# Quarter score products inside a level, and the last z projection one turn earlier, in a hybrid decoder block

## Chip, cores, metric

One NeuronCore of a Trainium2 chip. The time is the device time of one execution of the kernel in microseconds; the value before is the median of 3 runs.

## Reference, cut to what matters

One decoder layer (512 tokens, width 1024, 8 heads per mixer, all float32):

```python
proj = rmsnorm(x) @ w_in                      # q, k, v of both mixers, z, gates
# mixer A, per head: two score maps of 64-wide halves j of q and k
logits[j] = qa[:, j] @ ka[:, j].T + bias      # causal
w = softmax(logits[0]) - lam * softmax(logits[1])
oa = rmsnorm(w @ va)
# mixer B, per head: chunked gated delta rule, chunk 64
#   A = I + strict_lower(k k^T * decay); its inverse is applied, then a scan over chunks
ob = rmsnorm(delta_rule(qb, kb, vb)) * silu(zb)
mixed = sigmoid(g0) * (oa @ w_br_a) + sigmoid(g1) * (ob @ w_br_b)
x = x + mixed @ w_out
# then a gated MLP with a width-3 convolution, and a gated embedding term
```

## The kernel before

Every projection is a `gemm` of one 128-column chunk of weights. Weights and activations are each split into a high and a low part, so each of the 8 blocks of the inner dimension takes three products of 512 columns (L498). These three products are one **fill step**; a chunk is 8 steps. Weights stream through four buffers: SP loads a chunk, GpSimd (`both`) or ScalarE (`high`) makes the high part, GpSimd (`split`) the low part. All chunks stand in one fixed order (`Stream`), and each has a fixed PSUM bank out of four.

The mixers are worked off in **turns**. `turn(h)` does head h of mixer B (`delta`) and head h+1 of mixer A (`attention`), and as fill the projections that later turns need. `turn(-1)` has no `delta`. Turns 0 to 5 are the **middle turns** (both mixers, and projections for another head of A: `more_a`); turn 6 is the **late turn** (nothing more of A to project), turn 7 the **last turn** (no attention). Each engine has its own copy of the turn's order, written out by hand; semaphores join them. TensorE's copy places fill steps with `f.step(n)`, and the tuples `STEPS...` say how many go where: `early` (before the levels), `first` and `second` (within and behind a level), `scan`, `late`.

A turn on TensorE, in order:
- `scores(a, 0)` (L602), the products k k^T (L648) and q k^T (L657), `ob_sum` of the head before (L631), `turn_w(a, 0)` (L609), `scores(a, 1)`.
- Six **levels** n = 1 to 6 that double the size of the inverted blocks. Each has a product of 64x64 tiles (L678, at n = 6 L680) into bank 7, which ScalarE copies to `ui` (L1072), and a second product from `ui` and `xt` (L690, at n = 6 L692), from which VectorE makes the next `xi` (L1484) and, transposed, the next `xt` (L1487). `first[n-1]` fill steps stand between the two, `second[n-1]` behind the second.
- Behind levels 2 and 4: `turn_w` of the attention weights, one step, the next `scores`. Behind level 6: `k_turn` (L626).
- `v_mm` (L712), `turn_w(a, 3)`, `v_turn` (L590), and a scan of four token tiles (L723, L724, L727, L732, L735), with `attend` (L616) after the first tile and `oa_sum` (L743) after the third. Then the sums for q and k of the next head but one (L572).

The attention of one head goes through its four token tiles i one after the other, because its scores, their softmax and the transposed weights share banks 3 and 4: `scores` i on TensorE; `maxima` on VectorE (bias, L1355; row extremes, L1360); `softmax` on ScalarE (L959); `combine` on VectorE (L1370 to L1372), which makes `pr`; `turn_w` on TensorE; `keep_w` on ScalarE (L965), which makes `wT`, for which the next `scores` waits. `scores` i uses (i+1)*128 columns, twice: once with rows 0 to 63 of q and k, once with rows 64 to 127.

Other names: `vbt` (L1501) is the scaled value tile, made on VectorE at level 2; SiLU is finished on VectorE in L1401; `conv` is L1386 and L1390; `o_a` (L1554) ends a head of A; `finish_z` is L1574; `prep` (L1345) makes `qa` and `ka`; `ob_scaled` is signalled by L1565. The late turn has four chunks of fill (`LATE`). The last turn has `zb` of head 7 as its first chunk (`LAST`), then eight chunks of `mix_a`, the gated branch projections of mixer A; before it TensorE waits for all of `o_a` (`oa_done`).

## Time and profile before

| | |
|---|---|
| time, median of 3 runs | 1237.29 us (1236.37 to 1237.43) |
| the profiled execution | 1236.77 us, its span 1235.0 us |
| TensorE (PE) busy | 97% of the span |
| VectorE (DVE), ScalarE (ACT), GpSimd (POOL) busy | 56%, 44%, 50% |
| chain that ended last | PE 82%, DVE 10%, ACT 5% |
| DMA | 83 GB/s on the mean |

The middle turns run from 104.1 to 505.3 us, the late turn to 561.1, the last turn's scan ends at 628.2; then come the rest of the branch projections, the output projection, the MLP and the embedding term. PE is TensorE's matmul queue and PEld its weight loads. Float32 matmuls show two records each. A record's duration reaches past the start of the next one, since matmuls are pipelined: what a product costs is read from one start to the next start.

### The profile page before, as it was taken

What the parts mean: (1) busy time and instruction counts of PE and PEld (TensorE: products, weight loads), DVE (VectorE), ACT (ScalarE), POOL (GpSimd) and SP (SyncE); (2) the same over time, 40 slices, a digit from 0 to 9 for tenths busy, and PEclk for the clock granted to TensorE, in tenths of its full rate; (3) what the DMA queues carried; (4) which work ended last, traced back from release to release, by engine and by line L of the source; (5) the groups of instructions that cost most, each with busy time, mean ns of one, the idle gap of its engine ahead of it and who ended that gap; (6) DMA issues with size and microseconds to landing.
All of it is one profiled execution on the core that took longest, in us unless ns stands there. A gap on an engine that the chain in (4) does not pass through costs nothing.

```text
span 1235.0 us, 19086 instructions
## 1 busy us (share of the span) xinstructions
PE 1194.4 (97%) x6526; PEld 933.7 (76%) x6526; DVE 689.4 (56%) x1157; ACT 541.8 (44%) x926; POOL 615.8 (50%) x764
## 2 busy tenths in 40 slices
PE   5989999999999999989999999999999999999998
PEld 3766776767676777767788888888888888888886
DVE  4276667685858586777330242446677722751534
ACT  4254554555554645455242222454444422432542
POOL 5644354445343453425535564456666664574552
PEclk9989999999999999999999999999999999999999
DMA  8231212221212112211214352233433342332223
GB/s 256 76 95 53 61 52 61 69 61 53 61 52 78 52 35 78 69 35 52 69 51 120 85 176 79 86 93 94 120 94 94 101 121 69 102 100 87 66 84 89
DMA packets 192403, 102.65 MB, mean 83 GB/s; under 512 B 3798, under 2 KB 191177, under 8 KB 192329
## 3 DMA queue, kind: packets, MB, share of 16 engines
q1 hardware_dynamic: 191948, 101.55, 28.9%
q8 instruction: 41, 0.67, 0.2%
q14 instruction: 33, 0.27, 0.1%
q10 hardware_dynamic: 381, 0.15, 0.0%
HBM read 99.57 MB, written 2.13 MB: 82 GB/s over the span
## 4 chain that ended last, share of the span: by engine, by line
PE 82%; DVE 10%; ACT 5%; issue 2%; DMA 1%; SPq 0%; DVEq 0%; ACTq 0%
PE bank L498 68%; PE bank L602 2%; PE bank L678 2%; PE bank L690 1%; PE bank L616 1%; ACT junk_k L1040 1%; DVE qb L1401 1%; PE bank L609 1%; ACT silu L977 1%; PE bank L648 1%; PE bank L657 1%; ACT silu L978 1%; DVE ast L1360 1%; PE bank L631 1%; DVE ct L1414 1%
## 5 line engine op out<-in xcount | busy, mean ns | idle before, releaser
L435 POOL TENSOR_TENSOR w_lo<-w_raw,w_hi 128x256 fp32r<-128x256 f32 x692 | 543.7, 819 | 268.0 <-ACT w_hi L876 262.4
L498 PE MATMUL bank<-hn_hi,w_hi 128*128 128x512 f32 x1000 | 423.2, 423 | 0.0
L498 PE MATMUL bank<-hn_hi,w_lo 128*128 128x512 f32 x1000 | 391.9, 392 | 0.0
L498 PE MATMUL bank<-hn_lo,w_hi 128*128 128x512 f32 x1000 | 391.2, 391 | 0.0
L450 POOL CAST w_hi<-w_raw 128x1024 fp32r<-128x1024 f32 x68 | 72.2, 1062 | 334.7 <-PE bank L498 322.2
L498 PEld LDWEIGHTS bank<-hn_hi,w_hi 128*128 128x128 f32 x1000 | 188.4, 188 | 48.0 <-issue 11.2
L498 PEld LDWEIGHTS bank<-hn_hi,w_lo 128*128 128x128 f32 x1000 | 188.0, 188 | 41.2
L498 PEld LDWEIGHTS bank<-hn_lo,w_hi 128*128 128x128 f32 x1000 | 188.8, 189 | 37.1 <-issue 6.5
L876 ACT ACTIVATE w_hi<-w_raw 128x1024 fp32r<-128x1024 f32 x113 | 120.0, 1062 | 74.8 <-PE bank L498 66.6
L1689 DVE SCALAR_TENSOR_TENSOR u<-vr,pt,u 128x511 f32<-128x511 f32 x88 | 89.4, 1016 | 8.0 <-DVE vr L1683 0.3
L1683 DVE TENSOR_TENSOR vr<-bank,rs 128x512 f32<-128x512 f32 x44 | 30.4, 692 | 72.2 <-PE bank L498 67.1
L498 PE MATMUL bank<-fa_hi,w_hi 128*128 128x512 f32 x176 | 68.5, 389 | 0.0
L498 PE MATMUL bank<-fa_lo,w_hi 128*128 128x512 f32 x176 | 68.5, 389 | 0.0
L498 PE MATMUL bank<-fa_hi,w_lo 128*128 128x512 f32 x176 | 68.5, 389 | 0.0
L1206 ACT ACTIVATE u<-vr,pt 128x512 f32<-128x512 f32 x44 | 35.9, 816 | 38.4 <-DVEq L1684 37.6
L1072 ACT ACTIVATE ui<-bank 128x256 f32<-128x256 f32 (+1 forms) x48 | 18.4, 384 | 62.4 <-PE bank L678 56.1
L1723 DVE TENSOR_TENSOR x<-x,bank 128x512 f32 x16 | 11.0, 688 | 61.2 <-PE bank L498 60.5
L959 ACT ACTIVATE pr<-bank,ast 128x128 f32<-128x128 f32 (+3 forms) x64 | 33.8, 528 | 23.1 <-DVE ast L1360 21.1
L965 ACT ACTIVATE wT<-bank 128x128 f32<-128x128 f32 (+3 forms) x32 | 14.0, 438 | 67.9 <-PE bank L609 67.9
L1211 ACT ACTIVATE fa_hi<-tn 128x512 fp32r<-128x512 f32 x22 | 13.9, 633 | 65.6 <-DVE tn L1701 65.6
L678 PEld LDWEIGHTS bank<-xi,ct 64*64 64x64 f32 x640 | 22.0, 134 | 25.2 <-issue 14.0
L1626 DVE TENSOR_TENSOR sg<-sg,bank 128x512 f32<-128x512 f32 x8 | 5.5, 687 | 61.6 <-PE bank L498 61.6
(277 smaller groups left out, 1771.2 us busy)
## 6 DMA issues: line engine op xcount, KB each, us to landing
w_raw<-in_w_in SPq DMA_DIRECT2D x73, 512.0 KB, 3.9
w_raw<-in_w_up SPq DMA_DIRECT2D x44, 512.0 KB, 3.8
w_raw<-in_w_down SPq DMA_DIRECT2D x16, 512.0 KB, 3.9
w_raw<-in_w_br_a SPq DMA_DIRECT2D x8, 512.0 KB, 4.0
w_raw<-in_w_br_b SPq DMA_DIRECT2D x8, 512.0 KB, 3.9
w_raw<-in_w_out SPq DMA_DIRECT2D x8, 512.0 KB, 4.1
w_raw<-in_w_ple_gate SPq DMA_DIRECT2D x8, 512.0 KB, 4.1
w_raw<-in_w_down SPq DMA_DIRECT2D x8, 384.0 KB, 3.4
```

The costliest lines, as they stand in the source:

```text
L435: ins = pool.tensor_tensor(wlo[c.slot][:, ks, :], raw[c.slot][:, ks, :], whi[c.slot][:, ks, :].bitcast(F32), ALU.subtract)
L450: pool.tensor_copy(whi[c.slot][:, :, :], raw[c.slot][:, :, :]).then_inc(high_ready, 1)
L498: mm = pe.matmul(acc, w[c.slot][:, i, :], xx[:, x0 + i, :], start=(i == 0 and n == 0), stop=last)
L602: mm = pe.matmul(bank[3 + j][:, 0:(i + 1) * P], qa[s, i * P:(i + 1) * P], ka[s, 0:(i + 1) * P], start=True, stop=True)
L678: mm = pe.matmul(packed(7, 0, t, q), ct[n % 2][q, t, :], xi[q, t, :], start=True, stop=True)
L876: done(nc.scalar.activation(whi[c.slot][:, :, :], raw[c.slot][:, :, :], ACT.Copy), high_ready, c.number + 1)
L959: done(nc.scalar.activation(pr[j][:, 0:w], bank[3 + j][:, 0:w], ACT.Exp, bias=ast[:, 2 + j:3 + j], scale=-1.0, accum_out=ast[:, 4 + j:5 + j]),
L965: done(nc.scalar.activation(wT[:, 0:i + 1, i * P:(i + 1) * P], tiles(3)[:, 0:i + 1, :], ACT.Copy), "a_wT", h * 4 + (i + 1))
L1072: done(nc.scalar.activation(ui[q, :, :], packed(7, part=q), ACT.Copy), "ui", h * (NL - 1) + n)
L1206: done(nc.scalar.activation(u[:, :], v[:, :], ACT.Identity, bias=col(PA_FBIAS + q * KF, f), scale=col(PA_TAP[2] + q * KF, f)), "u_made", 2 ...
L1683: done(V.tensor_tensor(v[:, :], bank[c.bank][:, :], rs[:, :], ALU.mult), bank_free[c.bank], c.uses + 1)
L1689: link(V.scalar_tensor_tensor(out=u[:, back:], in0=v[:, 0:T - back], scalar=col(PA_TAP[j] + q * KF, f), in1=u[:, back:], op0=ALU.mult, op1 ...
```

## The change

In turns with both `delta` and `more_a` (named `tight`: turns 0 to 5), `scores` of token tiles 1, 2 and 3 stand between the two products of levels 1, 3 and 5, where fill steps stood, and each row half of a score is done as two products of 64 output partitions (`quarters`). The fill steps of that place go behind the second product. The softmax steps on ScalarE and VectorE move behind by about a level; `turn_w(a, 3)`, `v_turn`, `attend` and `oa_sum` move one scan tile back. `STEPS` gives four more steps behind levels 2 and 4 and four fewer at the turn's end.

The z projection of head 7 becomes a fifth chunk of the late turn (`zl`); `LAST` goes. The last turn's fill begins with `mix_a`, whose bank order becomes 2, 1, 3, 0; eight steps of a ninth chunk follow around `ob_sum`. TensorE's wait for `oa_done` ahead of the last turn goes. Of `mix_a`, GpSimd casts two more chunks and ScalarE two fewer. `low_a` does six blocks ahead of level 1, not four.

```diff
-STEPS = ((3, 2, 1, 1, 2), (2,) * 6, (1, 1, 1, 1, 1, 1), (3, (1, 1), (1, 1, 1), (1, 1, 1), (1, 1, 1)), (3, 6))
+STEPS = ((3, 2, 1, 1, 2), (2,) * 6, (1, 3, 1, 3, 1, 1), (3, (1, 1), (1, 1, 1), (1, 1, 1), (1, 1, 1)), (2, 3))
...
-STEPS_LATE = ((4, 2, 1, 1, 2), (2,) * 6, (0, 0, 0, 0, 0, 0), (2, (1, 0), (1, 0, 1), (1, 0, 1), (1, 0, 1)), (0, 0))
-STEPS_LAST = ((4, 4, 4, 2, 2), (3,) * 6, (3, 3, 3, 3, 3, 3), (3, (1, 1), (1, 1, 2), (1, 1, 2), (1, 1, 2)), (0, 0))
+STEPS_LATE = ((3, 2, 1, 1, 2), (2,) * 6, (1, 1, 1, 1, 1, 2), (3, (1, 0), (1, 0, 1), (1, 1, 1), (1, 1, 1)), (0, 1))
+STEPS_LAST = ((5, 2, 2, 2, 2), (3,) * 6, (3, 3, 3, 3, 3, 2), (2, (1, 1), (1, 1, 2), (1, 1, 1), (1, 1, 1)), (0, 0))
...
-LATE = ("qb", "kb", "vb", "zb")
-LAST = ("zb",)
+LATE = ("qb", "kb", "vb", "zb", "zl")
 HEAD_BANKS = (1, 0, 2)
-AHEAD = {"qa": 2, "ka": 2, "va": 2, "qb": 1, "kb": 1, "vb": 1, "zb": 0}
+AHEAD = {"qa": 2, "ka": 2, "va": 2, "qb": 1, "kb": 1, "vb": 1, "zb": 0, "zl": 1}
...
-        self.mix_a = Segment(self, KD // 2, slots, [2, 1, 0, 3])
+        self.mix_a = Segment(self, KD // 2, slots, [2, 1, 3, 0])
...
-            for n in range(4):
+            for n in range(len(LATE)):
                 both(stream.late.at(n))
-            both(stream.last.at(0))
-
-            for n in range(8 + 3):
+
+            for n in range(13):
                 both(stream.mix_a.at(n))
-            split(stream.mix_a.at(8 + 3))
-            for n in range(12, 16):
+            for n in range(13, 16):
...
+            def scores(h, i, quarters=False):
...
-                for j in range(2):
-                    s = slice(64 * j, 64 * j + 64)
-                    mm = pe.matmul(bank[3 + j][:, 0:(i + 1) * P], qa[s, i * P:(i + 1) * P],
-                                   ka[s, 0:(i + 1) * P], start=True, stop=True)
+                for j, s in enumerate((LOW, UP)):
+                    if not quarters:
+                        mm = pe.matmul(bank[3 + j][:, 0:(i + 1) * P], qa[s, i * P:(i + 1) * P],
+                                       ka[s, 0:(i + 1) * P], start=True, stop=True)
+                    else:
+                        for m, part in enumerate((LOW, UP)):
+                            at = i * P + m * HEAD
+                            mm = pe.matmul(bank[3 + j][part, 0:(i + 1) * P], qa[s, at:at + HEAD],
+                                           ka[s, 0:(i + 1) * P], start=True, stop=True)
                 mm.then_inc(sem("a_scores"), 1)
...
+                tight = delta and more_a
+                if attention and not tight:
                     scores(a, 1)
                 f.step(early[4])
...
                         mm.then_inc(sem("level_u"), 1)
-                    f.step(first[n - 1])
+                    joined = tight and n % 2 == 1
+                    if joined:
+                        scores(a, (n + 1) // 2, quarters=True)
+                    else:
+                        f.step(first[n - 1])
                     if delta:
...
                         mm.then_inc(sem("level_vt"), 1)
-                    f.step(second[n - 1])
+                    f.step(second[n - 1] + (first[n - 1] if joined else 0))
...
                     if n in (2, 4) and attention:
                         turn_w(a, n // 2)
                         f.step(1)
-                        scores(a, n // 2 + 1)
+                        if not tight:
+                            scores(a, n // 2 + 1)
                     if n == 6 and attention:
                         k_turn(a)
...
                 f.step(scan[0])
                 if attention:
-                    turn_w(a, 3)
-                    v_turn(a)
+                    if not tight:
+                        turn_w(a, 3)
+                        v_turn(a)
...
                     f.step(scan[1 + t][1])
-                    if t == 0 and attention:
+                    if t == 0 and tight:
+                        turn_w(a, 3)
+                        v_turn(a)
+                    if t == (1 if tight else 0) and attention:
                         attend(a)
-                    if t == 2 and attention:
+                    if t == (3 if tight else 2) and attention:
                         pe.wait_ge(sem("oa_sq"), a + 1)
                         pe.matmul(bank[4][:, :], ones, pr[1][:, :], start=True, stop=True).then_inc(sem("oa_sum"), 1)
...
-            pe.wait_ge(sem("oa_done"), H + 1)
-            fill = [gemm(stream.last.at(0), hn_hi, hn_lo)]
+            fill = []
             for n in range(2):
                 fill += [gemm(stream.mix_a.at(q, n), hn_hi, hn_lo) for q in range(2)]
                 fill += [gemm(stream.mix_a.at(2 + q, n), oa_hi, oa_lo, ready=("o_split", 0) if n + q == 0 else None)
                          for q in range(2)]
             turn(H - 1, None, fill, attention=False, more_a=False, steps=STEPS_LAST)
+            f = Fill(gemm(stream.mix_a.at(0, 2), hn_hi, hn_lo))
+            f.step(1)
             ob_sum(H - 1)
-
+            f.rest()
+            run(gemm(stream.mix_a.at(1, 2), hn_hi, hn_lo))
+            for q in range(2):
+                run(gemm(stream.mix_a.at(2 + q, 2), oa_hi, oa_lo))
...
-                    softmax(a, 1)
+                    if not tight:
+                        softmax(a, 1)
                 for n in range(1, NL):
+                    if tight and n in (3, 5):
+                        keep_w(a, n // 2)
...
                         if n == 2:
-                            keep_w(a, 1)
+                            if tight:
+                                softmax(a, 1)
+                            else:
+                                keep_w(a, 1)
                             silu_exp(a, 0)
...
                         if n == 4:
+                            if tight:
+                                softmax(a, 2)
                             act.wait_ge(sem("rows_read"), a + 1)
                             done(nc.scalar.activation(dec[:, :, :], dec[:, :, :], ACT.Exp), "dec", a + 1)
-                            keep_w(a, 2)
+                            if not tight:
+                                keep_w(a, 2)
                         if n == 5:
                             silu_exp(a, 1)
-                            softmax(a, 3)
+                            if not tight:
+                                softmax(a, 3)
                         if n == 6:
+                            if tight:
+                                softmax(a, 3)
                             first_tap(a, 2, at("vb"))
...
-                    if n in (1, 3) and not attention:
-                        gate_a(n // 2)
-                    if n == 2 and not attention:
-                        gate_z(h, at("zb"), attention)
+                    if n == 1 and not attention:
+                        gate_z(h, at("zl"), attention)
+                    if n in (2, 3) and not attention:
+                        gate_a(n - 2)
...
-                    high(seg.at(q + 3, n))
+                    if q < own:
+                        high(seg.at(q + 3, n))
+                if own == 0:
+                    act.wait_ge(low_ready, seg.at(5, n).number)
                 for q in range(2, 4):
                     high(seg.at(q + 3, n))
...
-                    low_a(range(4))
-                if attention:
+                    low_a(range(6))
+                if attention and not tight:
                     maxima(a, 1)
...
-                                link(V.transpose(xt[0:32, :, 32:64], xi[32:64, :, 0:32]))
+                                V.transpose(xt[0:32, :, 32:64], xi[32:64, :, 0:32])
                                 done(V.transpose(xt[64:96, :, 32:64], xi[96:128, :, 0:32]), "xt", h * NL + (n + 1))
...
                     if n == 1:
                         if attention:
-                            combine(a, 1)
+                            (maxima if tight else combine)(a, 1)
                             steps(conv(a, 0, at("qb")))
...
                         if attention:
-                            maxima(a, 2)
+                            if tight:
+                                combine(a, 1)
+                            else:
+                                maxima(a, 2)
                             steps(finish_silu(a, 0))
                     if n == 3 and attention:
+                        if tight:
+                            maxima(a, 2)
                         decay(a)
-                        combine(a, 2)
+                        if not tight:
+                            combine(a, 2)
                     if n == 4 and attention:
+                        if tight:
+                            combine(a, 2)
                         steps(conv(a, 1, at("kb")))
-                        maxima(a, 3)
+                        if not tight:
+                            maxima(a, 3)
                     if n == 5 and attention:
+                        if tight:
+                            maxima(a, 3)
                         steps(finish_silu(a, 1))
+                        if not tight:
+                            combine(a, 3)
+                    if n == 6 and tight:
                         combine(a, 3)
                     if n == 6 and h > 0:
                         finish_ob(h - 1)
                     if not attention:
-                        if n in (1, 2):
-                            low_a(range(2 * n + 2, 2 * n + 4))
+                        if n == 1:
+                            low_a(range(6, 8))
                         if n in (4, 5):
                             mix_a(n - 4, stream.mix_a.at(2 + n - 4), sqr[n - 4])
```

## Rows read from the trace of the kernel before

**Rows 1.** Busy time by stretch: busy us (instructions) per engine, clock, DMA share, GB/s
```profile
304.14:371.10 66.96, 66.02 (x448) 48.61 (x448) 47.91 (x95) 34.92 (x75) 29.52 (x35) 1.00 0.22 60
505.29:561.12 55.83, 47.98 (x372) 35.08 (x372) 41.18 (x85) 27.86 (x65) 19.60 (x23) 1.00 0.17 48
561.12:628.24 67.12, 66.93 (x448) 52.31 (x449) 34.86 (x61) 21.89 (x37) 35.44 (x43) 1.00 0.24 68
```

**Rows 2.** The chain that ended last, last turn: start us, length us, what
```profile
567.13 8.19 PE bank L498 x36
```

**Rows 3.** Timeline of PE, third middle turn: start us, us, engine, line, what, xcount, [idle before]
```profile
245.08 0.39 PE L498 MATMUL bank<-hn_hi,w_lo 128*128 128x512 f32 x1
245.40 0.70 PE L602 MATMUL bank<-ka,qa 64*128 64x256 f32 x4
246.03 0.50 PE L498 MATMUL bank<-hn_hi,w_hi 128*128 128x512 f32 x1
246.37 0.39 PE L498 MATMUL bank<-hn_lo,w_hi 128*128 128x512 f32 x1
...
249.82 0.68 PE L690 MATMUL bank<-ui,xt 64*64 64x64 f32 x16
...
251.77 0.68 PE L678 MATMUL bank<-xi,ct 64*64 64x64 f32 x16
...
256.39 0.92 PE L602 MATMUL bank<-ka,qa 64*128 64x384 f32 x4
257.24 0.68 PE L678 MATMUL bank<-xi,ct 64*64 64x64 f32 x16
257.85 0.50 PE L498 MATMUL bank<-hn_hi,w_hi 128*128 128x512 f32 x1
...
261.86 0.68 PE L678 MATMUL bank<-xi,ct 64*64 64x64 f32 x16 [0.83 <-DVE xi L1484]
...
271.36 0.68 PE L680 MATMUL bank<-xi,lt 64*64 64x64 f32 x8
```

**Rows 4.** The score line alone, 199.6 to 199.7 us: records, durations ns, starts
```profile
L602 PE MATMUL bank<-ka,qa x2: 693/693/693, 199.6 to 199.6; 64*128 64x512 f32 x2
```

**Rows 5.** Timeline of DVE, then of ACT, the same turn's levels 1 and 2
```profile
250.62 0.42 DVE L1484 TENSOR_TENSOR xi<-xi,bank 128x256 f32<-128x256 f32 x1 [2.17 <-PE bank L690]
...
252.20 0.48 DVE L1372 SCALAR_TENSOR_TENSOR pr<-pr,ast 128x256 f32<-128x256 f32 x1
...
256.58 0.69 DVE L1501 TENSOR_TENSOR vbt<-bank,kroot 128x512 f32<-128x512 f32 x1
...
252.56 0.38 ACT L1072 ACTIVATE ui<-bank 128x256 f32<-128x256 f32 x1 [3.12 <-PE bank L678]
```

**Rows 6.** Timelines of PE, ACT and DVE, the same turn's end; DVE of the late turn
```profile
280.62 2.32 PE L616 MATMUL bank<-wT,va 128*128 128x512 f32 x8
282.77 0.39 PE L723 MATMUL bank<-state,kb 128*128 128x128 f32 x2
...
286.03 0.49 PE L723 MATMUL bank<-state,kb 128*128 128x128 f32 x2
...
304.14 0.49 PE L602 MATMUL bank<-ka,qa 64*128 64x128 f32 x4
...
287.70 0.60 ACT L1111 ACTIVATE pr<-bank 128x512 f32<-128x512 f32 x1
...
296.16 0.75 DVE L1554 SCALAR_TENSOR_TENSOR o_a<-bank,sm,pr 128x512 f32<-128x512 f32 x1 [2.72 <-ACT pr L868]
...
299.20 1.11 DVE L1574 TENSOR_TENSOR zb<-zb,silu 128x512 f32<-128x512 f32 x1
...
563.58 0.69 DVE L1574 TENSOR_TENSOR zb<-zb,silu 128x512 f32<-128x512 f32 x1
```

**Rows 7.** Waits of PE, late turn: who waited for whom: us in total, times, longest
```profile
PE bank L678 <- DVE xi L1484: 2.9, 2, 2.7
PE bank L648 <- DVE o_a L1554: 1.4, 1, 1.4
```

More of the change, by code:

```diff
@@ L137, in __init__ @@
         self.late = heads(len(LATE))
-        self.last = heads(len(LAST))
         slots, four = [(self.count + i) % 4 for i in range(4)], [0, 1, 2, 3]
-        self.mix_a = Segment(self, KD // 2, slots, [2, 1, 0, 3])
+        self.mix_a = Segment(self, KD // 2, slots, [2, 1, 3, 0])
         self.mix_b = Segment(self, KD // 2, slots, four)
@@ L383, in _ @@
                 load(stream.late.at(n), w_in0, COLS[name] + (H - 2 + AHEAD[name]) * P)
-            load(stream.last.at(0), w_in0, COLS["zb"] + (H - 1) * P)
             for seg, gate, branch in ((stream.mix_a, COLS["g0"], bra0), (stream.mix_b, COLS["g1"], brb0)):
@@ L591, in v_turn @@
                 mm.then_inc(sem("va_T"), 1)
-            def scores(h, i):
+            def scores(h, i, quarters=False):
                 if i == 0:
@@ L775, in mix @@
                     run(gemm(seg.at(2 + q, n), hi, lo, ready=ready if q == 0 else None))
-            with pe.Fori(2, KD // 2) as n:
+            with pe.Fori(3, KD // 2) as n:
                 mix(stream.mix_a, n, oa_hi, oa_lo)
@@ L1054, in turn @@
                 a = h + 1
+                tight = delta and more_a
                 if not attention:
@@ L1077, in turn @@
                         if n == 2:
-                            keep_w(a, 1)
+                            if tight:
+                                softmax(a, 1)
+                            else:
+                                keep_w(a, 1)
                             silu_exp(a, 0)
                         if n == 3:
-                            softmax(a, 2)
+                            if not tight:
+                                softmax(a, 2)
                             first_tap(a, 1, at("kb"))
@@ L1089, in turn @@
                         if n == 4:
+                            if tight:
+                                softmax(a, 2)
                             act.wait_ge(sem("rows_read"), a + 1)
                             done(nc.scalar.activation(dec[:, :, :], dec[:, :, :], ACT.Exp), "dec", a + 1)
[L1092 removed]
+                            if not tight:
+                                keep_w(a, 2)
                         if n == 5:
                             silu_exp(a, 1)
[L1095 removed]
+                            if not tight:
+                                softmax(a, 3)
                         if n == 6:
+                            if tight:
+                                softmax(a, 3)
                             first_tap(a, 2, at("vb"))
[L1098 to L1101 removed]
+                    if n == 1 and not attention:
+                        gate_z(h, at("zl"), attention)
+                    if n in (2, 3) and not attention:
+                        gate_a(n - 2)
                 if not attention:
@@ L1149, in _ @@
             turn(H - 2, place(stream.late, LATE), more_a=False)
-            turn(H - 1, place(stream.last, LAST), attention=False, more_a=False)
+            turn(H - 1, place(stream.late, LATE), attention=False, more_a=False)
             ob_r(H - 1)
@@ L1157, in _, with mix @@
                 done(nc.scalar.activation(ob_hi[:, k, :], o_b[:, k, :], ACT.Copy), "o_high", H + k + 1)
-            act.wait_ge(low_ready, stream.mix_a.at(3, 2).number)
-            def mix(seg, n, made, used, ahead):
+            def mix(seg, n, made, used, ahead, own=2):
                 for q in range(2):
@@ L1167, in mix @@
                     act.sem_inc(sem(made), 1)
-                    high(seg.at(q + 3, n))
+                    if q < own:
+                        high(seg.at(q + 3, n))
+                if own == 0:
+                    act.wait_ge(low_ready, seg.at(5, n).number)
                 for q in range(2, 4):
                     high(seg.at(q + 3, n))
-            with act.Fori(2, KD // 2) as n:
+            mix(stream.mix_a, 2, "ga_made", "ga_used", 0, own=0)
+            with act.Fori(3, KD // 2) as n:
                 mix(stream.mix_a, n, "ga_made", "ga_used", 0)
@@ L1447, in turn @@
                 a = h + 1
+                tight = delta and more_a
                 if attention:
@@ L1503, in turn @@
                         if attention:
-                            maxima(a, 2)
+                            if tight:
+                                combine(a, 1)
+                            else:
+                                maxima(a, 2)
                             steps(finish_silu(a, 0))
                     if n == 3 and attention:
+                        if tight:
+                            maxima(a, 2)
                         decay(a)
-                        combine(a, 2)
+                        if not tight:
+                            combine(a, 2)
                     if n == 4 and attention:
+                        if tight:
+                            combine(a, 2)
                         steps(conv(a, 1, at("kb")))
-                        maxima(a, 3)
+                        if not tight:
+                            maxima(a, 3)
                     if n == 5 and attention:
+                        if tight:
+                            maxima(a, 3)
                         steps(finish_silu(a, 1))
+                        if not tight:
+                            combine(a, 3)
+                    if n == 6 and tight:
                         combine(a, 3)
```

3 lines of the change are left out of this document (1 added, 2 removed).

## The prediction

> **What bounds the kernel now.** I read the stretches first. A middle head turn (304.14 to 371.10) takes 66.96 us, of which TensorE is busy 66.02; the last turn (561.12 to 628.24) has it busy 66.93 of 67.12; the late turn before it (505.29 to 561.12) only 47.98 of 55.83 [rows 1]. The granted clock is 1.00 in all three. So the kernel is a TensorE queue: a microsecond counts if it is TensorE work, or a hole in that queue. The holes are 7.85 us in the late turn and 0.94 us in each middle turn.
>
> The unit of what follows is a fill step, three 512-column products of a projection. The chain that ended last shows 36 such products in 8.19 us [rows 2], so one starts 0.23 us after another and a step is 0.69 us.
>
> The timeline then shows what a change of the array's form costs. The last full-array product starts at 245.08, the 64-row score block (256 columns) at 245.40, the next full product at 246.03 and the one after at 246.37 [rows 3]: 1.29 us where two ordinary intervals take 0.46, so the block adds 0.83. The 384-column block runs from 256.39 to 257.24, 0.85 against 0.63, so 128 columns are 0.22 us and 256 are 0.44; 0.39, say 0.4 us, belongs to going in and out. A 64x64 level block also occupies 0.61 (257.24 to 257.85), and with its slow entry and exit adds 0.81, 0.4 of it again for the form. A score block that stands straight ahead of a level block (257.24) shares one entry and exit but pays 0.2 between 64x128 and 64x64.
>
> **The middle turns, part by part** (six of them, `tight`).
>
> *Forms.* Now: score 1 stands alone (0.4) and the two level-1 products alone (0.8); scores 2 and 3 are joined to the first product of levels 3 and 5 (0.6 each), the second products alone (0.4 each). Total 3.2 us. After: three blocks of level product, quarters, level product, each entered and left once: 1.2. Removed: 2.0 us a turn.
>
> *Quarters.* The columns stay 256, 384 and 512, but each row half is now two 64x64 matmuls. Today's two row halves overlap: two records of the score line start in the same tenth of a microsecond [rows 4]. Nothing in this trace has two products from the same row half into different column halves. Lower bound: all four overlap and streaming is as now, 0.44, 0.66 and 0.88. Upper bound for column halves that take turns: twice that. I take the lower, since the array does work as separate tiles: 16 level records in two tiles (257.24) take 0.68 us, as 8 records in one tile do (271.36) [rows 3].
>
> *The wait for `ui`.* The fill that lay between the level products is gone. A first product at 251.77 is followed by the `ui` copy at 252.56, 0.38 long [rows 5]: 1.17, with the release about 1.25 us. Level product plus quarters occupy about 0.52 + 0.44, + 0.66, + 0.88. So TensorE idles 0.3, 0.1 and 0: 0.4 us a turn. ScalarE is free then, because softmax 1 and 2 now stand behind their `ui`.
>
> *The old hole.* The wait of 0.83 at 261.86 [rows 3] was for `xi`, held up behind maxima and SiLU on VectorE; with three steps instead of one before that product it closes, and most of the turn's 0.94 with it: 0.9.
>
> *The new hole.* `turn_w(1)` now waits for `combine(1)`, which VectorE does only after level 2: 0.80 from the second product to `xi` (249.82 to 250.62), 2.06 for `xi`, `xt` and a two-tile combine (250.62 to 252.68), 0.69 for `vbt`, 0.15 of gaps [rows 3, 5]: 3.7 us after the product starts. TensorE gets there after 0.61 + 0.1 + 3 steps = 2.8. Hole 0.9. At level 4 there is no `vbt`, but combine has a third tile (0.2 more): 3.1, hole 0.3. Together 1.2. Queued behind it are `turn_w`, one step and the next level product.
>
> Up to the scan: 2.0 + 0.9 - 0.4 - 1.2 = 1.3 us gained a turn.
>
> *The tail.* Four fill steps (2.8 us) leave the turn's end for levels 2 and 4, and `turn_w(3)`, `v_turn` and `attend` move one scan step back. From `attend` (280.62) to the next turn's first scores (304.14) are 23.5 us; one scan tile (282.77 to 286.03, 3.26) moves ahead of it and four steps go, leaving 17.5 of which about 0.3 is today's wait: 17.2 of TensorE work. But a serial chain hangs on `attend`: its products 2.3, then ScalarE from the square (287.70) through norms, z gate, `qa` copy and reciprocal root to VectorE's `o_a` (296.16), 8.46, then VectorE alone until the next scores (296.16 to 304.14), 7.98, with gaps 18.9 us [rows 6]. Today the chain starts later, at 287.70 behind the third SiLU, and is hidden almost wholly. Afterwards it is longer than the work by 1.7, of which 0.3 was there before: 1.4 lost. VectorE's share can shrink: the z product there takes 1.11 against 0.69 in the late turn [rows 6], while GpSimd splits weights, and with the shifted fill some of four such operations fall outside: up to 1.1 less. I take 0.9 lost (0.3 to 1.4). SP and GpSimd keep the order of their chunks; nothing else moves.
>
> Net 0.4 us a turn, 2.4 for six (bounds 0 and 5.4 by the tail's ends and 0.3 for the holes).
>
> **The late turn and the last.** The z projection of the last head (8 steps, 5.6 us) leaves the last turn, which is full, and goes into the late one, with one more step taken from `mix_a`. The late turn's holes are waits for VectorE: 2.9 us for `xi` before L678, 1.4 for `o_a` before L648 [rows 7], the rest smaller ones. Seven more steps lie between level products and one fewer ahead of them. VectorE is the bound there, so they cost nothing by L712; a step ahead of the scan and one in its third tile cost 0.7 each, and everything behind, `o_a` too, comes 1.4 later. The removed `oa_done` wait lets L648 start at once; the next wait is L657's for `ob_scaled`, also 1.4 later than now. Nine steps (6.2 us) are done by then: 4.8 gained. If the added form changes (0.2 each, three places) don't hide it is 4.2; if the scan's holes absorb the shift, 5.6. The last turn keeps three steps between products; `low_a(6)` makes the second `xi` late by some 0.3, no more. Two weight casts move from ScalarE to GpSimd, about 1 us each, where GpSimd is busy 35.4 of 67.1 us [rows 1]: nothing.
>
> **Sum.** 1236.8 (the profiled execution; its span is 1235.0, the rest lies around it) - 2.4 - 4.8 = 1229.6. The median of the runs shown is 1237.3, 0.5 above the profiled one, so 1230.
>
> **Rivals.**
> *The column halves take turns.* Level product to level product would be 1.4, 1.8 and 2.3 us instead of 1.25, 1.25 and 1.4: 1.6 a turn, 9.6 in all, 1239 to 1240. For it: every pair that overlaps in the trace differs in its row half. Against: the score's row halves run independently, so the array does work as separate tiles.
> The Trainium skill ("TensorE: Matmul & The Clock Gate", Part 3, The mechanism) says that a weight load passes running matmuls only when the row group differs, which would give this rival's 1239. The same page's speedup table shows column packing working, and "TensorEngine Tiling (Array Packing)" (Tile-to-Partition Mapping) counts four independent 64x64 tiles, which would give 1230. No row here shows which.
>
> *The softmax chain costs more than the forms give (slower than before).* Place: `turn_w(1)` and `turn_w(2)` behind `combine`. The forms and the old hole give 2.5 net of `ui`; the tail takes 0.9. If the two holes together are 4.0 instead of 1.2 (VectorE reaching level 2's `xi` only after the query convolution, 2.3 us, as it does with today's order of work), each turn loses 2.4: 14.4 lost, 4.8 gained, about 1247. It decides for slower from holes of 2.8 a turn. Against: by the durations, VectorE ends that convolution 0.7 before the product it waits for.
>
> *The tail takes all of it.* With 1.4 lost there and holes of 1.2 to 1.6, the middle turns give nothing and only the late turn counts: 1232.5.
>
> **Chances.** My sum 0.58 (own range 1226 to 1234); tail takes all 0.14; column halves in turn 0.14; softmax chain 0.10; the late turn gives under 2 us, its fill colliding with VectorE's waits, 0.04. The range of 8 in 10 reaches from 1226 to 1240. A measurement of this kernel can't tell less than 0.2% (2.5 us) from no change. Faster than 1234.8: 0.72; within: 0.11; slower than 1239.8: 0.17.
>
> **What would show it.** Quarters: 4 + 4 records of the score line, and L678 to L690 at 1.25 us for levels 1 and 3; 1.8 at level 3 means turns. Forms: four entries into a 64-row form fewer a turn, and no 64x128 block beside a 64x64 one. New hole: a wait of L609 for `pr` of 0.9 at level 2, 0.3 at level 4; over 1.4 each, the softmax rival. Tail: the next turn's L602 waiting for `ka` 1 us rather than 0.3, perhaps part of it at the second L572. Late turn: its waits of TensorE down from 7.9 to 2.5 or less, last turn some 5 us shorter. The middle turn should be 66.5 us; 67 or more refutes my sign there.

## The result and the profile after

The changed kernel takes 1246.72 us (median of 4, 1246.09 to 1247.13), the kernel before in the same comparison 1236.83 (4 runs, 1235.41 to 1237.43): a ratio of 1.0076, 95% interval 1.0061 to 1.0091. It is 9.9 us slower where 1230 was forecast, and lies outside the forecast range of 1226 to 1240.

The page of the changed kernel, its first lines (busy us, share of the span, instructions):

```profile
span 1245.3 us, 19193 instructions
...
PE 1190.7 (96%) x6598; PEld 931.5 (75%) x6598; DVE 697.7 (56%) x1157; ACT 538.4 (43%) x923; POOL 619.9 (50%) x766
```

Its stretches in the order and with the columns of [rows 1]: a middle turn, the late turn, the last turn.

```profile
310.09:379.32 69.23, 65.38 (x460) 48.24 (x461) 49.00 (x95) 34.91 (x76) 29.41 (x36) 1.00 0.22 58
518.10:573.34 55.24, 53.36 (x397) 39.38 (x398) 38.98 (x83) 26.96 (x63) 21.48 (x26) 1.00 0.17 48
573.34:638.00 64.66, 62.09 (x430) 48.31 (x428) 36.70 (x63) 22.71 (x39) 34.27 (x41) 1.00 0.23 66
```

The middle turn grew from 66.96 to 69.23, yet TensorE is busy 0.64 less in it: the work shrank, and 3.85 us are now holes. VectorE does the same 95 instructions in 49.00 instead of 47.91. The late turn has 1.88 us of holes where it had 7.85; the last turn is 2.46 shorter, but has 2.57 us of holes where it had 0.19.

Who made TensorE wait, changed kernel, that middle turn (us in total, times, longest):

```profile
PE bank L609 <- DVE pr L1402: 2.7, 2, 1.6
PE bank L567 <- ACT sqr L930: 0.7, 1, 0.7
PE bank L597 <- DVE ka L1375: 0.2, 1, 0.2
PE bank L493 <- DVE vb L1420: 0.2, 1, 0.2
```

(Lines have moved: the gemm is L493, whole scores L597, quarters L602, the level products L679 and L695, `combine` L1400 to L1402.) `turn_w` waits for `combine` at levels 2 and 4, the place that the prediction names, 2.7 us by waits. Read from one start to the next, in the third middle turn, the holes are 3.0: the fill behind L695 starts at 257.82, L609 at 261.79, and nine products take 2.19 of these 3.97; that leaves 1.8, and at level 4 by the same working (269.82 to 273.24) 1.2. The prediction has 1.2 for both together.

TensorE, changed kernel, levels 1 to 3 of the third middle turn, the turn of [rows 3]:

```profile
250.46 0.62 PE L679 MATMUL bank<-xi,ct 64*64 64x64 f32 x13
250.87 0.43 PE L602 MATMUL bank<-ka,qa 64*64 64x256 f32 x1
...
250.98 0.60 PE L602 MATMUL bank<-ka,qa 64*64 64x256 f32 x6
251.69 0.68 PE L695 MATMUL bank<-ui,xt 64*64 64x64 f32 x16
...
257.21 0.68 PE L695 MATMUL bank<-ui,xt 64*64 64x64 f32 x16
...
259.77 0.39 PE L493 MATMUL bank<-hn_hi,w_lo 128*128 128x512 f32 x1
261.79 0.44 PE L609 MATMUL bank<-sq,pr 128*128 128x128 f32 x2 [1.63 <-DVE pr L1402]
...
262.86 0.62 PE L679 MATMUL bank<-xi,ct 64*64 64x64 f32 x14
263.26 0.54 PE L602 MATMUL bank<-ka,qa 64*64 64x384 f32 x2
```

Level product to level product is 1.23 (250.46 to 251.69): the quarters overlap as forecast. What made `combine` late stands on the next two engines. VectorE, then GpSimd, changed kernel, at the two places:

```profile
258.95 0.69 DVE L1532 TENSOR_TENSOR vbt<-bank,kroot 128x512 f32<-128x512 f32 x1
...
259.87 0.93 DVE L1401 TENSOR_SCALAR pr<-pr,ast,sm 128x256 f32<-128x256 f32 x1
260.84 0.90 DVE L1402 SCALAR_TENSOR_TENSOR pr<-pr,ast 128x256 f32<-128x256 f32 x1
...
271.14 1.04 DVE L1401 TENSOR_SCALAR pr<-pr,ast,sm 128x384 f32<-128x384 f32 x1
272.22 0.97 DVE L1402 SCALAR_TENSOR_TENSOR pr<-pr,ast 128x384 f32<-128x384 f32 x1
```

```profile
259.62 1.04 POOL L447 CAST w_hi<-w_raw 128x1024 fp32r<-128x1024 f32 x1 [5.73 <-PE bank L493]
260.73 3.59 POOL L432 TENSOR_TENSOR w_lo<-w_raw,w_hi 128x256 fp32r<-128x256 f32 x4
270.93 1.04 POOL L447 CAST w_hi<-w_raw 128x1024 fp32r<-128x1024 f32 x1 [6.61 <-PE bank L493]
272.05 3.10 POOL L432 TENSOR_TENSOR w_lo<-w_raw,w_hi 128x256 fp32r<-128x256 f32 x4
```

And the kernel before, VectorE's two operations and GpSimd's bursts on either side of them:

```profile
251.75 0.41 DVE L1371 TENSOR_SCALAR pr<-pr,ast,sm 128x256 f32<-128x256 f32 x1
252.20 0.48 DVE L1372 SCALAR_TENSOR_TENSOR pr<-pr,ast 128x256 f32<-128x256 f32 x1
```

```profile
248.25 2.87 POOL L435 TENSOR_TENSOR w_lo<-w_raw,w_hi 128x256 fp32r<-128x256 f32 x4
256.60 1.04 POOL L450 CAST w_hi<-w_raw 128x1024 fp32r<-128x1024 f32 x1 [5.47 <-PE bank L498]
```

Before, GpSimd was idle from 251.1 to 256.6 while `combine(1)` took 0.41 + 0.48. Now GpSimd starts a weight chunk at 259.62, released by TensorE, and `combine`, right behind it, takes 0.93 + 0.90. The release is the end of a chunk of fill, and the changed order lets one end within the steps just ahead of `turn_w`, at level 2 and again at level 4.

The kernel before had such a collision too, in another place. VectorE, then GpSimd, kernel before, ahead of its own wait of 0.83 at 261.86 [rows 3]:

```profile
259.28 1.10 DVE L1401 TENSOR_TENSOR qb<-qb,silu 128x512 f32<-128x512 f32 x1
260.41 0.85 DVE L1414 TENSOR_TENSOR ct<-lt,sq 128x256 f32<-128x256 f32 x1
```

```profile
257.71 3.27 POOL L435 TENSOR_TENSOR w_lo<-w_raw,w_hi 128x256 fp32r<-128x256 f32 x4
```

Where GpSimd rests, these two take 0.69 and 0.43 (258.09 of e3 below; 255.18 of the kernel before): 0.83 less together, as much as the whole wait. This is read from the rows; no run here holds GpSimd at that place alone.

**Where the time went**, by the starts of k k^T (L648), which each turn has once. Six middle turns: 104.54 to 505.71 before, 103.81 to 518.52 after, so 13.5 us longer. From there to the first product of the last branch projections (`ob`, 683.55 before, 693.87 after): 177.84 and 175.35, so 2.5 shorter. Behind that 551.45 and 551.43. The 0.7 at the start is the scatter of it: 103.1 to 104.9 in the kernels below.

### The profile page after: what moved, and what is told of

The parts are those of the page before. It is cut to its first block, busy times and chain, and to the rows that moved or that the text cites. A ratio compares the mean times of both kernels' runs of the same rounds, so it can differ in the third digit from the quotient of the medians.

```text
span 1245.3 us, 19193 instructions
## 1 busy us (share of the span) xinstructions
PE 1190.7 (96%) x6598; PEld 931.5 (75%) x6598; DVE 697.7 (56%) x1157; ACT 538.4 (43%) x923; POOL 619.9 (50%) x766
## 4 chain that ended last, share of the span: by engine, by line
PE 83%; DVE 12%; ACT 2%; issue 2%; DMA 1%; SPq 0%; DVEq 0%; ACTq 0%
PE bank L493 68%; PE bank L695 2%; PE bank L679 2%; PE bank L616 1%; DVE pr L1401 1%; DVE pr L1402 1%; PE bank L609 1%; PE bank L602 1%; PE bank L648 1%; PE bank L597 1%; DMA tab<-in_rel_bias 1%; DVE oa_lo L1625 1%; DVE xi L1515 1%; PE bank L657 1%; DVE first_x L1468 0%
## 5 line engine op out<-in xcount | busy, mean ns | idle before, releaser
L493 PE MATMUL bank<-hn_hi,w_hi 128*128 128x512 f32 x1000 | 423.4, 423 | 1.9 <-DVE o_a L1632 1.0
L493 PE MATMUL bank<-hn_hi,w_lo 128*128 128x512 f32 x1000 | 391.5, 392 | 0.0
L493 PE MATMUL bank<-hn_lo,w_hi 128*128 128x512 f32 x1000 | 391.2, 391 | 0.0
L493 PEld LDWEIGHTS bank<-hn_hi,w_hi 128*128 128x128 f32 x1000 | 188.3, 188 | 50.3 <-issue 13.4
L493 PEld LDWEIGHTS bank<-hn_hi,w_lo 128*128 128x128 f32 x1000 | 188.0, 188 | 41.1
L493 PEld LDWEIGHTS bank<-hn_lo,w_hi 128*128 128x128 f32 x1000 | 188.7, 189 | 39.7 <-issue 8.2
L493 PE MATMUL bank<-fa_hi,w_hi 128*128 128x512 f32 x176 | 68.5, 389 | 0.0
L493 PE MATMUL bank<-fa_lo,w_hi 128*128 128x512 f32 x176 | 68.5, 389 | 0.0
L493 PE MATMUL bank<-fa_hi,w_lo 128*128 128x512 f32 x176 | 68.5, 389 | 0.0
L1515 DVE TENSOR_TENSOR xi<-xi,bank 128x256 f32<-128x256 f32 x40 | 16.9, 421 | 47.5 <-PE bank L695 46.7
```

The costliest lines, as they stand in the source:

```text
L493: mm = pe.matmul(acc, w[c.slot][:, i, :], xx[:, x0 + i, :], start=(i == 0 and n == 0), stop=last)
L1515: done(V.tensor_tensor(xi[:, :, :], xi[:, :, :], packed(5), ALU.subtract), "xi", h * (NL - 1) + (n + 1))
```

## Experiments

Each is the changed kernel with one edit unless it says otherwise. Ratios are to the kernel before, run on the same chip (its medians: 1237.10 us beside e1 to e4, 1236.62 beside e5 to e8, 1238.45 beside e9 and e10, 1237.00 beside e11 and e12).

### e1_late_only: the late part alone

The middle turns in their old order, with the old `STEPS`.

```diff
-                tight = delta and more_a      # TensorE, ScalarE and VectorE
+                tight = False
```

> The late and last turns as changed, the middle turns as before (old order, old STEPS). If the loss lies in the middle turns alone: middle turns 66.9 to 67.0 us as before, and the kernel 3 to 4 us faster than before, 1233 to 1234. Rival, the move of the z projection itself costs something that the middle turns don't show: 1236 or more.

1232.67 us, ratio 0.9967 (0.9957 to 0.9977): 4.4 less than before, where 4.8 were forecast for the late part (by the spans of the two profiles, 1231.7 and 1235.0, it is 3.3). The traces divide these 3.3: the stretch from the late turn's L648 to the first `ob` product is 2.4 shorter (175.40 against 177.84), the six middle turns are 1.2 shorter (399.98), and the part ahead of them is 0.3 longer. So the late part alone is worth 2.4, half of the forecast.

### e2_middle_only: the middle part alone

The kernel before with only the middle turns' order, `STEPS` and quarters.

> The middle turns as changed, the late and last turns as before. If the two parts simply add: middle turns 69.2 us, 2.3 more than before, six of them, 13 to 14 us slower than before, about 1250. Rival, the two parts hinder each other: under 1246.

1251.28 us, ratio 1.0113 (1.0096 to 1.0130): 14.2 more. 14.2 - 4.4 = 9.8 is the whole change's 9.9. By the traces too the parts add up: the six middle turns take 414.41 (13.2 more than before), and 13.2 less the 2.4 of e1 is 10.8 where the changed kernel has 11.0 (13.5 - 2.5). The loss is in the middle turns.

The profiled execution of e2 spans 15.0 more than that of the kernel before, and 1.85 of it have another source: its late turn takes 57.26 (from k k^T to k k^T) where the same code took 55.41 before. Stretches of e2 (columns as in [rows 1]):

```profile
541.50:543.00 1.50, 0.00 (x0) 0.00 (x0) 1.47 (x2) 1.44 (x5) 1.50 (x3) 1.00 0.00 0
545.00:546.00 1.00, 1.00 (x3) 0.81 (x4) 0.93 (x4) 0.90 (x2) 0.00 (x0) 0.50 0.16 22
```

Behind a stop of 2.7 us for `xi` the granted clock of TensorE was at the lower of its two levels, 0.50 (1.2 GHz), for 6.8 us (about 543.2 to 550.1), and fill products there start 0.43 apart instead of 0.23. In the profiled execution of the kernel before the same stop left the clock at 1.00. Of the other executions of the kernel before, those with a mean clock of 0.992 to 0.994 took 1238.3 to 1240.4 us, those with 0.995 to 0.998 at most 1238.1; whether they had this fall isn't shown, since their traces aren't kept. In the changed late turn the longest stop is 0.9.

### e3_hold_gpsimd: GpSimd starts its bursts behind combine

```diff
                 for n in range(7):
+                    if n in (5, 6):
+                        pool.wait_ge(sem("a_w"), (h + 1) * 4 + n - 3)
+                    if n == 0 and h > 0:
+                        pool.wait_ge(sem("a_w"), h * 4 + 4)
                     both(...)
```

`a_w` counts `combine`; the third wait stands ahead of the burst at the turn's end. No work, and no step on the other engines, is changed.

> As changed, but GpSimd begins the sixth and seventh chunk of a middle turn and the first of the next only when combine(1), combine(2) and combine(3) are done. Theory A, combine is slow because GpSimd's weight split falls on it: L1401 and L1402 for two tiles fall from 0.93 and 0.90 to about 0.41 and 0.48, for three from 1.04 and 0.97 to 0.48 and 0.62, the two waits of L609 from 1.6 and 1.1 to 0.7 and 0.2, a middle turn from 69.2 to 67.4 and the kernel 10 to 11 us down, 1236. Theory B, combine comes late by its place alone, behind xi, xt and vbt: waits of L609 within 0.3 of now, kernel 1245 to 1247.

1236.21 us (10 runs), ratio 0.9990 (0.9981 to 1.0000): 10.5 less than the changed kernel. VectorE, then TensorE's waits (a middle turn), of this run:

```profile
257.13 0.41 DVE L1405 TENSOR_SCALAR pr<-pr,ast,sm 128x256 f32<-128x256 f32 x1
257.57 0.48 DVE L1406 SCALAR_TENSOR_TENSOR pr<-pr,ast 128x256 f32<-128x256 f32 x1
258.09 0.69 DVE L1435 TENSOR_TENSOR qb<-qb,silu 128x512 f32<-128x512 f32 x1
...
267.42 0.48 DVE L1405 TENSOR_SCALAR pr<-pr,ast,sm 128x384 f32<-128x384 f32 x1
267.94 0.62 DVE L1406 SCALAR_TENSOR_TENSOR pr<-pr,ast 128x384 f32<-128x384 f32 x1
```

```profile
PE bank L613 <- DVE pr L1406: 0.9, 2, 0.7
PE bank L571 <- ACT sqr L934: 0.7, 1, 0.7
```

`combine` is back at its old durations and the two holes measure 0.85 and 0.31 from start to start, the 0.9 and 0.3 of the prediction. The six middle turns take 402.65 (104.80 to 507.45), 12.1 less than in the changed kernel. So 12.1 of the middle turns' 13.5 are this collision (the two holes alone are 1.84 a turn, 11.0 in six), and without it they are still 0.25 longer each than before, not 0.4 shorter.

### e4_whole_products: no quarters

```diff
-                        scores(a, (n + 1) // 2, quarters=True)
+                        scores(a, (n + 1) // 2)
```

> As changed, but the scores between the level products are two whole 64x128 products, not four quarters. If quarters overlap and the form change costs 0.2 each way: level product to level product 1.3, 1.5 and 1.7 us instead of 1.23, 1.22 and 1.38, 0.6 a turn, 3 to 4 us slower than the changed kernel, about 1250. Theory C, the quarters are where the time went: level product to level product no longer, and the kernel no slower than the changed one.

1250.49 us, ratio 1.0114 (1.0097 to 1.0131), 3.8 more than the changed kernel. TensorE in this run, level 3:

```profile
263.32 0.68 PE L679 MATMUL bank<-xi,ct 64*64 64x64 f32 x16
263.94 0.92 PE L597 MATMUL bank<-ka,qa 64*128 64x384 f32 x4
264.78 0.68 PE L695 MATMUL bank<-ui,xt 64*64 64x64 f32 x16
```

1.46 from level product to level product against 1.22 with quarters (1.24, 1.46 and 1.67 at the three levels against 1.23, 1.22 and 1.38): the quarters pay 0.5 to 0.6 a turn, and the column halves don't take turns.

### e9_late_hold: the control

e1's kernel with the waits of e3.

> Control: the late part alone (old order of the middle turns) with the same three waits of GpSimd. In that order combine ends 4 to 5 us before GpSimd comes to these chunks, so the waits should find their count reached. If the hold only helps against the overlap that the new order made: within 1.2 us of the late part alone (1232.7). Rival, holding GpSimd helps any order: 1229 or less.

1233.08 us, ratio 0.9952 (0.9935 to 0.9968); the six middle turns take 400.14 against e1's 399.98. Where `combine` did not collide, holding GpSimd gives nothing: its gain in e3 is that of the collision and not a general one.

### e5_hold_order and e6_hold_steps: what remains of the holes

e5 is e3 with `combine(1)` ahead of `vbt` on VectorE. e6 is e3 with its fill shifted towards the waits:

```diff
-STEPS = (..., (1, 3, 1, 3, 1, 1), ..., (2, 3))
+STEPS = (..., (1, 4, 0, 3, 0, 1), ..., (2, 4))
```

> The version with the held GpSimd, and combine(1) ahead of vbt on VectorE. If the rest of the first wait is the place behind vbt (0.69 us): the wait of L609 at level 2 goes from 0.7 to about 0, a middle turn is 0.6 to 0.7 us shorter, the kernel 4 us below the held one, about 1232. Rival, the wait has another source (softmax 1 on ScalarE ends too late for it): no change over 1 us.

1231.07 us, ratio 0.9954 (0.9936 to 0.9972). The wait of L613 for `pr` falls from 0.9 to 0.2 a turn and the turn from 67.07 to 66.37: six turns take 4.3 us less, as the removed 0.7 says; the medians, from two comparisons, differ by 5.1.

> The version with the held GpSimd, with second = (1, 4, 0, 3, 0, 1) and late = (2, 4): one fill step more ahead of turn_w(1) and one more between the two sums of q and k, two fewer behind levels 3 and 5. Theory, the first 0.7 of the level-2 wait and of the tail's waits (0.7 at the second sum, 0.3 at the next scores) are free places, and the places behind levels 3 and 5 are not: 1.2 to 1.4 us a turn shorter, 1228 to 1229. Rival, the tail is not bound by the chain behind attend, so the moved steps only change their place: 1234 or more.

1227.01 us, ratio 0.9919 (0.9902 to 0.9936). The turn takes 65.7, 1.4 less than in e3: the hole at L613 shrinks by 0.7, and with one step more in the tail its wait for `sqr` (0.7) is gone, while the one for `ka` grows from 0.2 to 0.6. So the tail was short of work, and levels 3 and 5 gave up their steps without a wait. The time is 1.0 below the expected range.

### e7_low4: the second xi of the last turn

`low_a` in two portions again, four blocks ahead of level 1.

> As changed, but low_a does four blocks ahead of level 1 and two each behind levels 1 and 2, as before. If six blocks were what made the second xi of the last turn late: the product behind L704 starts 0.5 to 0.6 us after it, not 2.1, and the span is about 1.5 us shorter, 1244; a part of up to 0.4 may come back at the first branch chunk, which waits for the last blocks.

1248.76 us (one execution), 2.0 above the changed kernel's median: the expectation fell. The hole at the second `xi` goes, a bigger one comes. TensorE, changed kernel, then this run:

```profile
594.12 0.68 PE L679 MATMUL bank<-xi,ct 64*64 64x64 f32 x16 [1.48 <-DVE xi L1515]
```

```profile
599.14 0.50 PE L493 MATMUL bank<-oa_hi,w_hi 128*128 128x512 f32 x1 [2.52 <-DVE oa_lo L1625]
```

The fill itself needs these blocks: without the z chunk at its head, the last turn comes to the products of `oa` 8 steps sooner. From the late turn's L648 to the first `ob` product are 176.52 us instead of 175.35, and e8, with four blocks too, has 176.50 where e10 has 175.33. So six blocks ahead of level 1 are the cheaper place, by 1.2 us.

### e8, e10: the mended orders together

e8 has e3's waits, e5's order, the steps (1, 3, 0, 3, 1, 1) and (2, 4), and e7's `low_a`; e10 the same without e7 and with e6's steps.

> Held GpSimd, combine(1) ahead of vbt, low_a as before, and one fill step from behind level 3 to between the sums of q and k: second = (1, 3, 0, 3, 1, 1), late = (2, 4). If the four terms add (10.5, 4, 4 and 1.5 us off the changed kernel): 1226 to 1228, faster than before and than the late part alone (1232.7). Rival, the turn is bound by VectorE as a whole once the waits are short: 1230 to 1232.

> Held GpSimd, combine(1) ahead of vbt, second = (1, 4, 0, 3, 0, 1), late = (2, 4), low_a(6) as changed. The held version with these steps (1227.0) still waits 0.2 us a turn at L609, and the earlier combine can take away no more than that: 1225.5 to 1227. Rival, the order still gives its own 5 us: 1222.

e8: 1227.80 us, ratio 0.9928 (0.9910 to 0.9945). e10: 1224.48 us, ratio 0.9888 (0.9871 to 0.9904), 14.0 us faster than before (12.6 by the spans of the profiles, 1222.4 and 1235.0). e8 lies in its expected range, but partly by luck: the 1.5 us that the expectation took for `low_a` are a cost of 1.2. e10 lies 1.0 below its range: its middle turn is 65.43 where e6, without the earlier `combine(1)`, has 65.70, though both wait 0.2 at L613. A middle turn of e10 (columns as in [rows 1]), then TensorE's waits in it:

```profile
298.58:364.01 65.43, 64.48 (x462) 48.33 (x460) 46.03 (x95) 34.92 (x75) 28.77 (x36) 1.00 0.22 61
```

```profile
PE bank L601 <- DVE ka L1379: 0.6, 1, 0.6
PE bank L613 <- DVE pr L1406: 0.2, 1, 0.2
```

TensorE's busy time is 1.54 below that of [rows 1], and the turn 1.53 shorter.

### e11_after_banks and e12_best_banks: a hole behind the turns

Behind the last turn the changed kernel has a wait which the kernel before has not:

```profile
682.89 0.47 PE L493 MATMUL bank<-hn_hi,w_hi 128*128 128x512 f32 x1 [0.98 <-DVE o_a L1632]
```

With `mix_a` in the bank order 2, 1, 3, 0 its last product and the first of `mix_b` (0, 1, 2, 3) use the same bank. Before, `mix_a` ended on bank 3.

```diff
-        self.mix_b = Segment(self, KD // 2, slots, four)
+        self.mix_b = Segment(self, KD // 2, slots, [1, 0, 2, 3])
```

> The changed kernel with one edit: the second mixing segment takes its banks in the order 1, 0, 2, 3 in place of 0, 1, 2, 3, so that its first product no longer writes the bank which the last product of the first mixing segment has just filled. In the changed kernel TensorE stands 0.98 us at 682.89, at the start of the second segment, for VectorE's copy out of that bank (L1632, 0.69 long, at 682.05); in the kernel before that boundary has no hole. If the bank is the cause, the hole goes and nothing else moves: about 1.1 us less than the changed kernel, 1245.6. If the hole comes from the later arrival of something else (weights, the gate), it stays and the time is 1246.7.

> The version with GpSimd held, combine(1) ahead of vbt and the steps (1, 4, 0, 3, 0, 1) and (2, 4), with the same bank order for the second mixing segment. The hole of 1 us at the boundary of the segments is in that version too. Expected: 1223.4, 1.1 less than 1224.5, ratio to the kernel before about 0.988. With the other cause 1224.5.

e12 is e10 with the same edit. e11: 1245.71 us, ratio 1.0067 (1.0046 to 1.0087), 1.0 below the changed kernel. The wait is gone, and from the last `ob_sum` (L631) to the end are 606.1 us instead of 607.3. e12: 1224.76 us, ratio 0.9898 (0.9878 to 0.9919). Its wait is gone too, but its total isn't below e10's: the two intervals overlap, and e12's profiled run began its turns 1.1 us later (104.18 against 103.10). The expected 1223.4 didn't come. The mend is shown in the trace, its worth on top of e10 is not.

## Why the prediction was wrong

**The step that failed: the new hole.** The prediction has "a two-tile combine (250.62 to 252.68)" in its 3.7 us and finds holes of 0.9 and 0.3. That duration was read where GpSimd was idle. In the new order the fill steps just ahead of `turn_w` finish a chunk, GpSimd starts on the next weights, and `combine` takes 1.83 instead of 0.89 (2.01 instead of 1.10 at level 4). The holes are 3.0 instead of 1.2, and e3 takes 10.5 us away with nothing but later bursts. A middle turn was forecast 0.4 shorter and came out 2.26 longer; 1.8 of this miss of 2.7 are the holes, 0.7 the tail (below). The rule was at hand: the prediction itself used the slowed z product of the tail, 1.11 against 0.69 [rows 6], as a gain. It said "SP and GpSimd keep the order of their chunks; nothing else moves" and did not ask when they would start.

The prediction's own row for the old hole, 0.83, was such a collision as well; it gave maxima and SiLU as the reason and did not ask why SiLU took 1.10.

The rows show more than a slow-down: `combine`'s first operation ends at 260.80, 0.14 behind the cast (259.62 + 1.04), and its second at 261.74, close behind the first of the four subtractions (0.72 each alone). In e3, where VectorE's SiLU product starts first (258.09), it keeps its 0.69 and the cast at 258.12 takes 1.56:

```profile
258.12 1.56 POOL L447 CAST w_hi<-w_raw 128x1024 fp32r<-128x1024 f32 x1 [6.95 <-DVE pr L1406]
```

So in these rows who starts first keeps its time and the other waits. The Trainium skill ("SBUF — State Buffer", Who interferes with whom) says that a VectorE operation with two SBUF inputs contends with a GpSimd one that reads SBUF, that one in a two-port mode does so too, and that the order of issue decides who blocks. The trace agrees on who waits, not quite on how much: the first operation ends 0.14 behind the cast, where its own 0.41 would still lie ahead of it. Nor is the collision gone in e3: VectorE's next operation there, `ct` (L1448 at 258.82), takes 1.14 instead of 0.43. It stands where TensorE doesn't wait for it.

**The tail** was mis-sized. From the value product to the next turn's scores there were 28.61 us before (L712 to L602) and 27.42 after with 2.78 less fill: 1.6 lost, where 0.9 was taken and 1.4 was the upper end. TensorE, changed kernel, the third middle turn:

```profile
290.80 0.47 PE L493 MATMUL bank<-hn_hi,w_hi 128*128 128x512 f32 x1 [0.16 <-DVE vb L1420]
291.57 2.32 PE L616 MATMUL bank<-wT,va 128*128 128x512 f32 x8
306.02 1.12 PE L567 MATMUL bank<-sqr,sq 128*128 128x512 f32 x2 [0.70 <-ACT sqr L930]
```

The chain was sized well: from `attend` (291.57) to the next scores (310.09) are 18.52, where 18.9 was said. The work beside it, by the prediction's own way of counting, is 23.52 - 3.26 - 2.78 = 17.48, so 1.0 is lost there, near the 0.9. The other 0.55 lies ahead of `attend` (8.90 from the value product, where 5.09 + 3.26 were due), mostly at a stop for `vb` which the prediction doesn't have: 0.16 as a wait, 0.55 from the product ahead of it (L742, 290.25) to 290.80 where the other three of that kind have 0.14 to 0.17. e6, with one fill step more, has 0.8 of waits in the turn, 0.6 of them in the tail.

**The late turn and the last** gave 3.7 (to the start of the last block of `oa` products, 661.79 before and 670.86 after: 156.08 and 152.34 from L648 of the late turn) instead of 4.8. The waits of TensorE in the last turn, changed kernel, show why:

```profile
PE bank L679 <- DVE xi L1515: 1.5, 1, 1.5
PE bank L657 <- DVE o_b L1610: 1.1, 1, 1.1
PE bank L742 <- DVE vbt L1582: 0.5, 1, 0.5
```

The second `xi` costs 1.5 where 0.3 was said (1.2 more, about the shortfall of 1.1), and L657's wait is that which the prediction named. Then the bank order of `mix_a`, which the prediction did not look at, takes 1.2 back: that last block takes 12.03 instead of 10.88. Together 2.5. The late turn itself did as forecast (holes from 7.85 to 1.88); the last turn is 2.5 shorter, not some 5.

**What held.** The busy time of the middle turn fell; level to level is 1.23, 1.22 and 1.38 where 1.25, 1.25 and 1.4 were given; the wait for `xi` of 0.83 [rows 3] is gone; the place of the new hole; the sign of the late part. With combine uncontended (e3) the holes are the predicted ones.

**A sum that doesn't come out.** The prediction's bounds for six middle turns, 0 and 5.4, don't follow from its terms: 1.3 less a tail of 0.3 to 1.4 gives -0.6 to 6.0, and with 0.3 for the holes -2.4 to 7.8. Even the low end is far from the 13.5 lost.

**The rivals.** Column halves in turn: refuted by the 1.22 at level 3, and by e4. Slower by the softmax chain: its place, its threshold (2.8 a turn, measured 3.0) and its time (1247) came out, but not its mechanism, since VectorE starts `xi` at 258.01, 0.80 after L695 at 257.21, and not behind the convolution. Its 0.10 was too little for a place where two holes hung on durations taken from one setting. The tail takes all: the tail lost even a little more than this rival's 1.4, and with `combine` uncontended (e3) the middle turns do give nothing; its 1232.5 missed the collision as the sum did. The late part under 2 us: it gave 2.4 to 2.5.

**Left open.** e1's middle turns, whose order is that of before, are 0.2 us shorter each (66.80 against 66.96, 1.2 in all). In the fourth of them the difference lies at the value product, which needs `xf` of VectorE: from L626 to the first fill product behind the value product 0.58 us pass (341.73 to 342.31), before 0.80 (341.95 to 342.75), where the value product starts 0.06 behind the end of `xf`. Ahead of it the SiLU product of k takes 0.69 in e1 and 1.29 before, while `combine(3)` and one GpSimd subtraction are the longer ones: another order in the same collision. One wait between two transposes on VectorE is dropped in e1 and starts this product 0.03 sooner in the turn; that this turns the order round is likely, but no run tests it. Why the mended turns gain 0.27 from the earlier `combine(1)` (e10 against e6) was not taken apart either.

## What to carry to other kernels

When a chain is moved, look not only at what it waits for but at what it will then run beside: an engine released by TensorE's progress moves with the fill, and a VectorE duration holds only for the neighbour that it was read beside. If the other engine has slack (GpSimd is busy under half of each middle turn here), let it wait for the end of the urgent operation; here that was worth 10.5 us of 1247. Where one segment's banks are reordered, look at the bank on which the next one starts.

## What the runs showed of the hardware

- VectorE's operations on SBUF alone, scalar and two-input ones, took 1.6 to 2.3 times as long beside GpSimd's cast and subtractions: 0.41 to 0.93, 0.48 to 0.90, 0.48 to 1.04, 0.62 to 0.97 us. Those that read PSUM and SBUF did not: the convolution L1416 at 273.22, two in 1.53, beside the subtractions of 272.05 to 275.15, and 1.53 too at 252.72 before, where GpSimd was idle.
- Four 64x64 products that share row halves in pairs overlap: with a level product they take 1.23 us at 256 columns and 1.22 at 384 to the next level product, where the prediction's sum for column halves in turn is 1.8 at 384.
- A stop of 2.7 us was followed by 6.8 us at the lower clock in e2 (0.50, products 0.43 apart instead of 0.23), and by none in the profile of the kernel before.
